# Where the four slots of split weights begin in SBUF: one place for each slot and part, in place of two places chosen by stage

## What is computed

```python
hproj = x @ w_in                       # retention: 1024 -> 6144
y = (o * jax.nn.silu(gate)) @ w_out    # 2048 -> 1024
c = x @ w_down; kv = (lat @ w_up)      # latent attention: 1024 -> 576, 512 -> 4096
q = (_rms_norm(q_lat, q_norm) @ w_uq)  # 768 -> 3072
u = h @ w_in                           # hybrid layer
merged = gates[:, :, 0] * (y_rnn @ w_o_rnn) + gates[:, :, 1] * (y_attn @ w_o_attn)
x = x + merged @ w_out
x = x + jnp.square(jax.nn.relu(h2 @ w_ff_in)) @ w_ff_out
```

## Time and profile before

| | |
|---|---|
| runs | 879.35, 880.38, 881.2 us; median 880.38 us |
| profiled execution | span 878.7 us from its first to its last instruction; it has no time of its own beside the span, and the three runs lie 0.7 to 2.5 us above that |
| TensorE matmul busy | 874.0 us, 99% of the span, 5577 matmuls |
| TensorE weight load busy | 780.4 us, 89% |
| VectorE, ScalarE, GpSimd busy | 607.8, 496.1, 101.9 us |
| chain that ended last | PE 98%, DMA 1%, DVE 1% |
| granted TensorE clock | full in all 40 slices |

### The profile page before, as it was taken

The page is one execution under the profiler, slowest core; times in us unless marked ns, Lnnn a source line. Parts: engine busy times, 40 slices in busy tenths (PEclk is TensorE's granted clock), DMA queues, the critical chain, the costliest instruction groups (busy, mean ns, idle before and its releaser), DMA issues.

```text
span 878.7 us, 13316 instructions
## 1 busy us (share of the span) xinstructions
PE 874.0 (99%) x5577; PEld 780.4 (89%) x5577; DVE 607.8 (69%) x838; ACT 496.1 (56%) x638; POOL 101.9 (12%) x50
## 2 busy tenths in 40 slices
PE   9999999999999999999999999999999999999998
PEld 8798887888999999999888899999999888888887
DVE  5976566659886777777568787778967766664442
ACT  6544445445666666666337667997753565554330
POOL 0110101000010000000000000224000035551000
PEclk9999999999999999999999999999999999999999
DMA  9934554642744444455474544324445655555520
GB/s 348 368 117 176 192 197 185 195 150 81 256 164 142 150 152 153 150 191 194 182 255 150 220 158 166 124 96 145 144 145 205 227 181 183 186 185 203 195 90 25
DMA packets 25116, 154.31 MB, mean 176 GB/s; under 512 B 3168, under 2 KB 3808, under 8 KB 9440
## 3 DMA queue, kind: packets, MB, share of 16 engines
q1 hardware_dynamic: 23312, 148.97, 47.1%
q10 hardware_dynamic: 1584, 3.96, 1.5%
q0 software_dynamic: 160, 0.52, 0.2%
HBM read 152.39 MB, written 1.05 MB: 175 GB/s over the span
## 4 chain that ended last, share of the span: by engine, by line
PE 98%; DMA 1%; DVE 1%; ACT 0%; SPq 0%; issue 0%; ACTq 0%
PE ps L389 25%; PE ps L391 25%; PE ps L390 25%; PE ps L480 6%; PE ps L483 3%; PE ps L707 1%; PE ps L496 1%; DMA a_first<-in_k_part 1%; PE ps L732 1%; PE ps L712 1%; PE ps L874 1%; PE ps L902 1%; PE ps L613 1%; PE ps L533 1%; PE ps L891 1%; PE ps L722 1%
## 5 line engine op out<-in xcount | busy, mean ns | idle before, releaser
L1542 DVE TENSOR_TENSOR w_lo_ring<-w_raw,w_hi_ring 128x2048 fp32r<-128x2048 f32 x145 | 332.3, 2303 | 151.5 <-ACT w_hi_ring L1079 151.0
L1079 ACT ACTIVATE w_hi_ring<-w_raw 128x2048 fp32r<-128x2048 f32 x145 | 276.6, 1917 | 119.6 <-PE ps L391 113.3
L389 PE MATMUL ps<-xT_hi,w_hi_ring 128*128 128x256 f32 x488 | 138.8, 284 | 0.0
L390 PE MATMUL ps<-xT_lo,w_hi_ring 128*128 128x256 f32 x488 | 136.6, 280 | 0.0
L391 PE MATMUL ps<-xT_hi,w_lo_ring 128*128 128x256 f32 x488 | 136.5, 280 | 0.0
L389 PE MATMUL ps<-w_hi_ring,xT_hi 128*128 128x512 f32 (+1 forms) x240 | 95.1, 396 | 0.0
L389 PEld LDWEIGHTS ps<-xT_hi,w_hi_ring 128*128 128x128 f32 x488 | 92.1, 189 | 1.9 <-issue 0.8
L391 PE MATMUL ps<-w_hi_ring,xT_lo 128*128 128x512 f32 (+1 forms) x240 | 92.8, 387 | 0.0
L390 PEld LDWEIGHTS ps<-xT_lo,w_hi_ring 128*128 128x128 f32 x488 | 92.1, 189 | 0.6
L390 PE MATMUL ps<-w_lo_ring,xT_hi 128*128 128x512 f32 (+1 forms) x240 | 92.6, 386 | 0.0
L391 PEld LDWEIGHTS ps<-xT_hi,w_lo_ring 128*128 128x128 f32 x488 | 92.1, 189 | 0.0
(11 more groups left out here) (337 smaller groups left out, 1755.9 us busy)
## 6 DMA issues: line engine op xcount, KB each, us to landing
w_raw<-in_a_w_in SPq DMA_DIRECT2D x21, 1024.0 KB, 5.0
w_raw<-in_w_ff_in SPq DMA_DIRECT2D x16, 1024.0 KB, 4.9
w_raw<-in_w_ff_out SPq DMA_DIRECT2D x16, 1024.0 KB, 4.8
w_raw<-in_b_w_uq SPq DMA_DIRECT2D x16, 576.0 KB, 4.3
w_raw<-in_a_w_out SPq DMA_DIRECT2D x8, 1024.0 KB, 4.8
w_raw<-in_b_w_gate SPq DMA_DIRECT2D x8, 1024.0 KB, 4.9
w_raw<-in_kv_w_up SPq DMA_DIRECT2D x8, 1024.0 KB, 4.8
w_raw<-in_b_w_out SPq DMA_DIRECT2D x8, 1024.0 KB, 4.8
```

Source lines behind the costliest of these rows:

```text
L389: k.T.matmul(out, lh, rh, start=start, stop=False, skip_group_check=True)
L390: k.T.matmul(out, lh, rl, start=False, stop=False, skip_group_check=True)
L1079: k.A.activation(k.hi[:, in_slot(u)], k.raw[u % RING][:, :], ACT.Copy).then_inc(k.s["w_hi"], 1)
L1542: k.V.tensor_tensor(k.lo[:, in_slot(u)], k.raw[u % RING][:, :], k.hi[:, in_slot(u)].bitcast(F32), ALU.subtract).then_inc(k.s["w_lo"], 1)
```

## The change

Both parts of all units get fixed places: slot r of the high parts begins at 8192 r + (0, 16, 64, 128) bytes, slot r of the low parts at 8192 r + (0, 32, 96, 224) bytes. `w_lo_ring` itself moves 128 bytes on, to a place that is 256 mod 512; `w_hi_ring` stays. All that lies behind the rings moves by 512 bytes, so that its places modulo 512 stay; the small buffers between the rings move by 96 bytes. `w_head`, its six waits on ScalarE and its six counts on TensorE go. No instruction is added, taken away or moved on any engine, and shapes stay as they are.

Begins modulo 512 bytes, for slots 0 to 3, where the activations begin at 160:

| | before, shifted | before, not shifted | now |
|---|---|---|---|
| high parts | 160, 160, 160, 160 | 128, 128, 128, 128 | 128, 144, 192, 256 |
| low parts | 160, 160, 160, 160 | 128, 128, 128, 128 | 256, 288, 352, 480 |
| high parts, distance to the activations | 0 | -32 | -32, -16, +32, +96 |
| low parts, distance to the activations | 0 | -32 | +96, +128, +192, +320 |

```diff
-SHIFT = 8
+BEGIN_HI = (0, 4, 16, 32)
+BEGIN_LO = (0, 8, 24, 56)
...
-def shifted(u):
-
-    return u < U_PAIR or U_BOUT <= u < U_RNNX or u >= U_WOUT
-
-
-def in_slot(u, cols=slice(0, SLOT)):
-
-    at = u % RING * SLOT + (SHIFT if shifted(u) else 0)
+def in_slot(u, begin, cols=slice(0, SLOT)):
+
+    at = u % RING * SLOT + begin[u % RING]
     return slice(at + cols.start, at + cols.stop)
...
+def in_hi(k, u, cols=slice(0, SLOT)):
+    return k.hi[:, in_slot(u, BEGIN_HI, cols)]
+
+
+def in_lo(k, u, cols=slice(0, SLOT)):
+    return k.lo[:, in_slot(u, BEGIN_LO, cols)]
...
-def heads_before(u):
-
-
-    return sum(1 for v in range(U_PAIR, u - 2) if head_signals(v)) if head_signals(u - 3) else 0
-
-
-def head_signals(v):
-    return v >= 0 and not shifted(v) and shifted(v + 3) and (v + 3) % RING != RING - 1
...
-    k.hi = k.place("w_hi_ring", [P, RING * SLOT + SHIFT], F32R)
+    k.hi = k.place("w_hi_ring", [P, RING * SLOT + BEGIN_HI[-1]], F32R)
...
-    k.top = k.at["w_hi_ring"] + RING * SLOT * 4 + 512
-    k.lo = k.place("w_lo_ring", [P, RING * SLOT + SHIFT], F32R)
+    k.top = k.at["w_hi_ring"] + RING * SLOT * 4 + 640
+    k.lo = k.place("w_lo_ring", [P, RING * SLOT + BEGIN_LO[-1]], F32R)
+    k.top = k.at["w_hi_ring"] + 2 * RING * SLOT * 4 + 1056
...
@@ feature_major
-                if n == 0 and c == 0 and head_signals(u):
-                    m.then_inc(k.s["w_head"], 1)
...
@@ act_hi
-    if heads_before(u):
-        k.A.wait_ge(k.s["w_head"], heads_before(u))
-    k.A.activation(k.hi[:, in_slot(u)], k.raw[u % RING][:, :], ACT.Copy).then_inc(k.s["w_hi"], 1)
+    k.A.activation(in_hi(k, u), k.raw[u % RING][:, :], ACT.Copy).then_inc(k.s["w_hi"], 1)
...
@@ dve_lo
-    k.V.tensor_tensor(k.lo[:, in_slot(u)], k.raw[u % RING][:, :], k.hi[:, in_slot(u)].bitcast(F32), ALU.subtract).then_inc(
+    k.V.tensor_tensor(in_lo(k, u), k.raw[u % RING][:, :], in_hi(k, u).bitcast(F32), ALU.subtract).then_inc(
```

More of the change, by code:

```diff
@@ L63 @@
 SEMAPHORES = (
-    *(f"w_landed{r}" for r in range(RING)), "w_hi", "w_lo", "w_used", "w_head",
+    *(f"w_landed{r}" for r in range(RING)), "w_hi", "w_lo", "w_used",
     *(f"x_in{n}" for n in range(len(PARTS))), "k_in0", "w_first0", "w_first1", "first_hi", "first_lo", "x_hi", "x_lo", "warm_in", "res_x", "ident_in", "ropeA_in", "decay_in", "lnw0_in", "lnw1_in", "tablesB_in", "columns_in", "kw_in",
@@ L128, in piece, with by_tiles @@
     return slice(2 * n, 2 * n + 2)
-def shifted(u):
-    return u < U_PAIR or U_BOUT <= u < U_RNNX or u >= U_WOUT
-def in_slot(u, cols=slice(0, SLOT)):
-    at = u % RING * SLOT + (SHIFT if shifted(u) else 0)
+def in_slot(u, begin, cols=slice(0, SLOT)):
+    at = u % RING * SLOT + begin[u % RING]
     return slice(at + cols.start, at + cols.stop)
-def in_tiles(ring, u, tiles):
-    return ring[:, in_slot(u, columns(tiles))].rearrange("p (k s) -> p k s", s=S)
-def heads_before(u):
-    return sum(1 for v in range(U_PAIR, u - 2) if head_signals(v)) if head_signals(u - 3) else 0
-def head_signals(v):
-    return v >= 0 and not shifted(v) and shifted(v + 3) and (v + 3) % RING != RING - 1
+def in_hi(k, u, cols=slice(0, SLOT)):
+    return k.hi[:, in_slot(u, BEGIN_HI, cols)]
+def in_lo(k, u, cols=slice(0, SLOT)):
+    return k.lo[:, in_slot(u, BEGIN_LO, cols)]
+def by_tiles(weights):
+    return weights.rearrange("p (k s) -> p k s", s=S)
 class Kernel:
@@ L400, in parts @@
 def parts(k, u, nk, cols):
-    return [z[:, in_slot(u, slice(0, nk * cols))].rearrange("p (k n) -> p k n", k=nk) for z in (k.hi, k.lo)]
+    return [ring(k, u, slice(0, nk * cols)).rearrange("p (k n) -> p k n", k=nk) for ring in (in_hi, in_lo)]
 def token_major(k, u, xT, k0, nk, cols, outs, first, last, ready=None):
@@ L759, in pe_pair @@
                         tuple(z[:, 3 * n + c, :] for z in k.b_qlatT), n == 0 and c == 0 and q != 1, n == 1 and c == 2)
-                if q == 0 and c == 0 and head_signals(u + 1 + n):
-                    m.then_inc(s["w_head"], 1)
         m.then_inc(s["w_used"], 1)
@@ L773, in pe_pair @@
                     tuple(z[:, c, :] for z in k.b_latT), h == 0 and c == 0, c == 3)
-            if h == 0 and c == 0 and head_signals(u + 3):
-                m.then_inc(s["w_head"], 1)
     if pair:
@@ L1086, in act_first @@
         k.A.wait_ge(k.s["k_in0"], 16)
-    k.A.activation(in_tiles(k.hi, u, tiles), k.a_first[:, tiles, 1 + u, :], ACT.Copy).then_inc(k.s["first_hi"], 1)
+    k.A.activation(by_tiles(in_hi(k, u, columns(tiles))), k.a_first[:, tiles, 1 + u, :], ACT.Copy).then_inc(k.s["first_hi"], 1)
 def act_piece(k, n):
@@ L1093, in act_piece @@
     cols = columns(piece(n))
-    k.A.activation(k.hi[:, in_slot(2, cols)], k.raw[2][:, cols], ACT.Copy).then_inc(k.s["first_hi"], 1)
+    k.A.activation(in_hi(k, 2, cols), k.raw[2][:, cols], ACT.Copy).then_inc(k.s["first_hi"], 1)
 def act_turned(k, name, pair, bank, hi, weight=None):
@@ L1549, in dve_first @@
     k.V.wait_ge(k.s["first_hi"], first_count(u, n))
-    k.V.tensor_tensor(in_tiles(k.lo, u, tiles), k.a_first[:, tiles, 1 + u, :], in_tiles(k.hi, u, tiles).bitcast(F32), ALU.subtract).then_inc(
+    k.V.tensor_tensor(by_tiles(in_lo(k, u, columns(tiles))), k.a_first[:, tiles, 1 + u, :],
+                      by_tiles(in_hi(k, u, columns(tiles))).bitcast(F32), ALU.subtract).then_inc(
         k.s["first_lo"], 1)
@@ L1556, in dve_piece @@
     k.V.wait_ge(k.s["first_hi"], first_count(2, n))
-    k.V.tensor_tensor(k.lo[:, in_slot(2, cols)], k.raw[2][:, cols], k.hi[:, in_slot(2, cols)].bitcast(F32), ALU.subtract).then_inc(
+    k.V.tensor_tensor(in_lo(k, 2, cols), k.raw[2][:, cols], in_hi(k, 2, cols).bitcast(F32), ALU.subtract).then_inc(
         k.s["first_lo"], 1)
```

## The result

The changed kernel takes **889.61 us** (median of 4 runs, 888.97 to 890.48) against 880.62 (879.35 to 881.2) for the kernel before in the same job: ratio 1.0107, 95% interval 1.0095 to 1.0119. It is slower by 9.0 us; the forecast was 875.2, its range 866 to 887, so both the value and the range are wrong. The profiled execution has a span of 887.7 us, 9.0 more than the one before.

The account below looks back on a forecast made before the run. TensorE's matmul pace was taken as the bound, with no wait or transfer to gain. Streamed weights -2.5, feed-forward -1.7, queries and keys -1.0, the rest 0: -5.2 us from 880.4 gave 875.2 us, overall range 866 to 887.

Parts of the forecast that it names:

- What bounds the kernel, waits, conversions: Whole kernel: TensorE's pace sets the time; dropping the semaphore waits and moving ScalarE's conversions each cost or gain 0.
- Weights streamed: 1578 matmuls leaving distance 0 gain 1.6 ns each, 2.5 us less; bounds 21.0 us less to 6.0 more.
- the sign of being wrong: Streamed starts 230 ns or more apart at 809 us and later, where all were 226.7, would refute the largest term.
- 13.3 ns lost, whatever the width: At distance 0, held 256-column and settled streamed 512-column matmuls were both read as losing 13.3 ns against pure streaming.
- Units at -32: Hybrid gates and head pairs, 2352 matmuls: no change taken; at worst 3.3 ns each, 7.8 us more.
- Queries and keys: Retention layer: 288 matmuls gain 3.3 ns each, 1.0 us less; bounds 3.8 us less to 0.
- Feed-forward, first half: 512 held matmuls leaving distance 0 gain 3.3 ns each, 1.7 us less; bounds 7.4 less to 1.7 more.
- The pattern is lost: Rival, chance 0.34: mixed distances keep streamed matmuls from settling at 226.7 ns; 5.0 us more, 885.4 us.
- its point of decision: The slower rival wins when the mean of the streamed matmuls rises by more than about 1.7 ns.
- Only the begin counts: Rival: the weights' begin within 64 bytes sets the pace, not distance; about 880.2 us; no-change case, chance 0.16.
- The reads come fully apart: Rival, chance 0.08: a distance of a quarter of 512 bytes or more frees both reads; 16 us less, 864 us.

Follow-up runs that it names:

- e12: Changed kernel, low parts placed like high ones, activations 320 bytes later, distances +160, +192, +224, +288 in slots 0 to 3: 890.39 us.
- e13: Kernel before, with held weights of hybrid gates and head pairs at -192 in place of -32, all others at 0: 876.07 us, ratio 0.9959.
- e1: Changed kernel with high and low parts of all units at one distance, -32, in every slot: 887.07 us, ratio 1.0082.
- e3: Changed kernel with the low parts at the same distances as the high ones (-32, -16, +32, +96): 890.15 us, ratio 1.0116.
- e2: Changed kernel with high and low parts of all units at distance 0 in every slot: 886.09 us, ratio 1.0071.
- e8: Kernel before with one more stage at -32, the first half of the feed-forward layer: 879.65 us, ratio 0.9996.
- e6: Kernel before, only the low parts of the squared feed-forward activations moved, in eight groups 0 to 384 bytes later: 881.51 us, ratio 1.0017.
- e5: Kernel before, squared feed-forward activations, high and low parts alike, moved in eight groups 0 to 384 bytes later, weights unmoved: 881.97 us, ratio 1.0022.
- e7: Kernel before, squared feed-forward activations, high and low alike, moved in eight groups 0, 4, 8 to 28 bytes later: 881.76 us, ratio 1.0019.
- e9: Changed kernel, low parts placed like high ones, distances -32, -28, -20, -8 in slots 0 to 3: 890.87 us, ratio 1.0126.

## Why the prediction was wrong

*What bounds the kernel, waits, conversions* (0 and 0): right. The waits are 2.0 us, a conversion takes 1914 ns in the mean against 1917, and all 9 us are pace. One premise was misread: `w_head` is counted up by L391, the last matmul of the first product, and not by L389, so that L389 ends no wait says nothing. What does: in the trace of the kernel before ScalarE sits idle before none of the six conversions (from 397.9, 399.7, 403.0, 662.3, 668.5 and 674.6 us on). The Trainium skill, "SBUF — State Buffer", section "Who interferes with whom", says "PE and ACT never wait on anyone"; the runs do not agree as far as TensorE's own two reads go: e12 and e13 hold the same matmuls, in the same order, 14 us apart, and 233.3 against 226.7 ns are seen where every other engine and the DMA are idle (e1).

*Weights streamed* (-2.5 taken, bound +6.0): **this is the step that failed.** It measured +6.9, and the sign of being wrong that the prediction named, 230 ns or more apart from 809 us on, is what the trace shows (232.5). I took the price from values of the head pairs at -32, 256 columns wide, which are 1.4 ns better than 120, and carried it, raised to 1.6, to 512 columns. e1 shows the two widths part at that very distance: 118.3 ns for 256 columns, 233.2 for 512, 5.8 ns *dearer* than at 0. "13.3 ns lost, whatever the width" was a finding at distance 0 alone. The bound was short too: I took 231.1, the pace of matmuls on their way to the settled pattern, for the worst one, while others never on that way run at 233.3 or, in e3, 236.7.

*Units at -32* (0 taken, +7.8 at most): sign not seen. With 2135 x 1.5 = 3.2 us they are the second term of the loss, and every slot has a share (118.7, 118.1, 118.0, 118.8 ns); with all of them at 0 it is 6.1 (e2). The +2.1 of all held matmuls, further up, is less because queries and keys gain and gaps are in it. The prediction had said that they go to other distances and still priced these like the one they left.

*Queries and keys* (-1.0): mechanism right, size off; 119.8 to 118.7 ns, 370 x 1.2 = 0.4 us less. 116.7 was the price of -32 alone, and e1 has it there.

*Feed-forward, first half* (-1.7): measured +0.3. Wide ones gained 1.9 ns and narrow ones lost 3.2; even at -32 throughout (e8) it is 0.4 us, not 1.7, since a price of held matmuls in rows of one width doesn't hold where widths alternate.

*The rivals.* "The pattern is lost" had the right place and the right sign; the mean of the streamed matmuls rose by 4.9 ns, past its point of decision, 1.7. Its price of 885.4 left out held weights and ended at 231.1, so it fell 4 us short. Its reason holds only in half: e6 shows that one matmul in three at another distance slows its neighbours too, but e1, without any mixing, loses as much. "Only the begin counts" fell to e5 and e13. "The reads come fully apart" found no distance for it; at the best, -192, held weights recover 3.4 of the 10 ns that -32 loses, and only in part of their stretches.

*What stays open:* what at a stretch's begin decides between 113.3 and 117.8 ns at -192, why -16 has several paces, and what in the memory or the reads makes these places. The runs show distances and paces, no cause below them. 0 for streamed weights is the best that was seen, not one proved best: distances between the steps of 32 were tried only near 0, -32 and -192, and +64 not at all.

## What to carry to other kernels

Where TensorE is the chain, add up starts, not durations, by kind of matmul, and look at the operands' begins modulo 512: here the same matmuls took 876 to 891 us by them alone. A price read at one distance and one width is a price for that distance and width; before a change moves operands to places that no row shows, take the worst pace seen as likely as the best. Tune each kind by itself (streamed at 0, held at -192 here), by a scan in which one buffer moves and everything else stays.

## What was not expected of the hardware

- The pace depends on the distance down to 4 bytes: 226.7 ns at 0, 232.3 at -4, 229.8 at -12 for 512 columns (e7); 116.9 at -32 (e1, e3, e9) and 119.8 at -28 (e9) for 256 columns held.
- The matmuls of a product do not have each its own pace: one of them at -32 raises the mean of the three from 226.7 to 232.9 ns (232, 238.5 and 228 to 229), at -128 or +128 to 231 (227, 233 and 234), at -256 or -16 not at all (e6).
- One distance can have two steady paces, 113.3 and 117.8 ns at -192, kept through stretches of 24 to 48 matmuls (e13), and both are left and met again within one kernel, in the same way in five executions as far as their times tell (within 0.4 us).
- 113.3 ns is the fastest held pace seen, 6.7 above the 106.7 of 256 columns at 2.4 GHz; the settled streamed pace, 226.7, is 13.3 above its 213.3.
